# A two-layer recurrent decoder kernel: history rows stacked before they are transposed, unread products of constants on TensorE, and layer norms that scale in one step

## The reference

```
x = layer_norm(ALPHA * x + 0.5 * swiglu(x, ffn1), ln1)
p = x @ w_in
ya, shift, wkv = rwkv7(p[..., :RWKV_COLS], state_shift, state_wkv, ...)
yb, conv, C, n, m = mlstm(p[..., RWKV_COLS:], state_conv, state_C, state_n, state_m, ...)
x = layer_norm(ALPHA * x + concat(ya, yb) @ w_out, ln2)
x = layer_norm(ALPHA * x + 0.5 * swiglu(x, ffn2), ln3)

layer_norm(x, g, b): mu = mean(x); var = mean((x - mu)**2)
                     return (x - mu) * rsqrt(var + LN_EPS) * g + b
```

## Time and profile before

| | |
|---|---|
| runs | 1639.57, 1639.91, 1642.65 us |
| median | 1639.91 us |
| the profiled execution's own time | 1636.58 us |
| its span, first to last instruction | 1634.5 us |
| TensorE busy | 1549.8 us (95%) |
| VectorE, ScalarE, GpSimd busy | 865.3, 665.4, 416.1 us |
| mean granted TensorE clock | 0.965 of 2.4 GHz |

### The profile page before, as it was taken

How to read it: one execution, slowest core, us unless ns; L and a number is a source line. 1 busy time by engine, 2 the same in 40 slices (tenths; PEclk the granted TensorE clock), 3 DMA queues, 4 the chain that set the end, 5 groups by cost and what they waited for, 6 DMA issues and landing times.

```text
span 1634.5 us, 34807 instructions
## 1 busy us (share of the span) xinstructions
PE 1549.8 (95%) x13868; PEld 1486.7 (91%) x13868; DVE 865.3 (53%) x1347; ACT 665.4 (41%) x1071; POOL 416.1 (25%) x427
## 2 busy tenths in 40 slices
PE   7999999999998899999899999999999998999994
PEld 7999998998977799999799999989978787999993
DVE  4444436686356764444464444366944577444334
ACT  4333235656432443333343333357563245333323
POOL 6222552013121432221052221020132324222011
PEclk9999999999997899999999999999999899999997
DMA  7455552442122555544354545434330443544420
GB/s 205 144 151 150 160 152 71 124 112 75 28 62 78 149 147 148 154 143 153 103 147 144 151 143 165 118 96 111 96 76 3 115 119 108 164 143 152 148 97 32
DMA packets 307200, 197.75 MB, mean 121 GB/s; under 512 B 7516, under 2 KB 282320, under 8 KB 307096
## 3 DMA queue, kind: packets, MB, share of 16 engines
q1 hardware_dynamic: 303512, 189.64, 39.9%
q0 software_dynamic: 3584, 6.62, 1.6%
HBM read 187.46 MB, written 8.78 MB: 120 GB/s over the span
## 4 chain that ended last, share of the span: by engine, by line
PE 89%; DVE 5%; ACT 3%; POOL 1%; DVEq 1%; issue 1%; DMA 0%; ACTq 0%; POOLq 0%
PE bank L1905 25%; PE bank L1907 24%; PE bank L1906 24%; PE bank L674 1%; PE bank L690 1%; PE bank L585 1%; PE bank L686 1%; PE bank L561 1%; PE bank L1976 1%; POOL xl L2349 1%; PE bank L423 1%; DVE x L2250 1%; PE bank L1978 1%; PE bank L433 1%; DVE z L2248 1%
## 5 line engine op out<-in xcount | busy, mean ns | idle before, releaser
L1905 PE MATMUL bank<-xh,whi 128*128 128x320 f32 x2016 | 632.8, 314 | 31.6 <-POOL xl L2379 24.7
L2217 DVE TENSOR_TENSOR wlo<-raw,whi 128x1024 fp32r<-128x1024 f32 x340 | 428.2, 1262 | 401.2 <-ACT whi L2101 400.5
L1906 PE MATMUL bank<-xl,whi 128*128 128x320 f32 x2016 | 628.5, 312 | 0.0
L1907 PE MATMUL bank<-xh,wlo 128*128 128x320 f32 x2016 | 628.2, 312 | 0.0
L2101 ACT ACTIVATE whi<-raw 128x1024 fp32r<-128x1024 f32 x340 | 359.2, 1060 | 573.9 <-PE bank L1907 569.4
L1905 PEld LDWEIGHTS bank<-xh,whi 128*128 128x128 f32 x2016 | 383.6, 190 | 38.4 <-issue 32.6
L1906 PEld LDWEIGHTS bank<-xl,whi 128*128 128x128 f32 x2016 | 383.8, 190 | 0.5
L1907 PEld LDWEIGHTS bank<-xh,wlo 128*128 128x128 f32 x2016 | 383.4, 190 | 0.0
L2359 POOL TENSOR_TENSOR hl<-scratch,hh 128x320 f32 x88 | 146.1, 1661 | 435.9 <-DVE scratch L2270 435.9
L1905 PE MATMUL bank<-hh,whi 128*128 (+1 forms) x704 | 218.4, 310 | 0.7 <-ACT vec L2137 0.7
L1907 PE MATMUL bank<-hh,wlo 128*128 (+1 forms) x704 | 217.2, 309 | 0.0
(11 more groups left out here) (363 smaller groups left out, 1568.0 us busy)
## 6 DMA issues: line engine op xcount, KB each, us to landing
raw<-in_ffn_wg SPq DMA_DIRECT2D x88, 512.0 KB, 3.8
raw<-in_ffn_wu SPq DMA_DIRECT2D x88, 512.0 KB, 3.8
raw<-in_ffn_wd SPq DMA_DIRECT2D x88, 512.0 KB, 3.6
raw<-in_w_in SPq DMA_DIRECT2D x60, 512.0 KB, 3.8
raw<-in_w_out SPq DMA_DIRECT2D x16, 512.0 KB, 5.4
raw<-in_state_C SPq DMA_DIRECT2D x8, 512.0 KB, 6.5
out_s_C<-raw SPq DMA_DIRECT2D x8, 512.0 KB, 3.5
ring<-in_state_wkv POOLq DMA_DIRECT2D x2, 1024.0 KB, 8.5
```

The lines of the kernel that those rows point to most:

```text
L1905: pe.matmul(out, w_hi, hi, start=start, stop=False)
L1906: pe.matmul(out, w_hi, lo, start=False, stop=False)
L1907: return pe.matmul(out, w_lo, hi, start=False, stop=stop)
L2217: dve.tensor_tensor(wlo[:, slot, :], raw[:, slot, :], whi[:, slot, :].bitcast(F32), ALU.subtract).then_inc(lo_ready.sem, 1)
```

## The change

Five things change.

1. *Norms.* The matrix of ones in the sums becomes `means`, filled with 1/1024. ACT squares the mean (a new step behind `stats_ready`), DVE makes the variance from it in one operation and floors it in a second. The mean is subtracted from six tiles in three operations of 640 columns. Gain and 1/sqrt are applied in one DVE operation; ACT makes `xh` by adding the bias; DVE, not POOL, makes `xl` in one operation from z, bias and `xh`. x itself is made by ACT, all eight tiles behind the eight of `xh`. For the very last norm no `xh` and `xl` are made.
2. *first_chunks.* PE goes on with six products of a tile as soon as `xh` is there, and makes the three with `xl` one tile later. `gates_product` and `residual` wait for all of x.
3. *Unread products.* `keep_array_busy` makes products of `ident` and `headones` that nobody reads: 18 in each norm but the last of all (4, then 9 behind `var_ready`, then 5 behind `rstd_ready`), and 18 in each layer's recurrence.
4. *History.* It is loaded as 112 and twice 96 rows of 128 and turned by 3 products where 22 stood.
5. *Last rows.* `tails` and `ends` are laid out so that 1 and 2 transposes turn them. The side steps are 24, at growth steps 0 to 5 and 9 to 26, none is left in the recurrence. The stores go out in three conv pieces where two stood.

```diff
+        def keep_array_busy(pe, b, n):
+
+            for _ in range(n):
+                pe.matmul(bank[b][:, 0:P], ident[:, :], headones[:, :], start=True, stop=True)
+
         def gates_product(pe, L):
 
             pe.wait_ge(gatew_in.sem, gatew_in.by(L, 64))
+            pe.wait_ge(xf_ready.sem, xf_ready.by(L, KT))
...
+        SIDE_AT = [*range(KEYS), *range(KEYS + 3, NSIDE + 3)]
...
             if k < VALUES:
-                for i, n in enumerate(range(4 * k, min(4 * k + 4, NRW))):
-                    last = pe.transpose(b[0:SB + 1, i * P:(i + 1) * P], tails[:, n, :], ident[:, :])
+                last = pe.transpose(b[0:(SB + 1) * NRW, 0:P], tails[:, :, :].rearrange("p s n -> p (s n)"), ident[:, :])
...
             elif k < MEMS:
-                for i in range(4):
-                    last = pe.transpose(b[0:LEAD * (SB + 1), i * P:(i + 1) * P],
-                                        ends[:, 4 * (k - ENDS) + i, :, :].rearrange("p s j -> p (s j)"), ident[:, :])
+                for i, (s0_, s1_) in enumerate(END_ROWS):
+                    last = pe.transpose(b[0:(s1_ - s0_) * END_BLOCK, i * P:(i + 1) * P],
+                                        ends[:, s0_:s1_, :, :].rearrange("p s j n -> p (s j n)"), ident[:, :])
...
             for j in range(NJ):
+                keep_array_busy(pe, 7, 2)
                 for b in range(SB):
...
                         samples_u(pe, L)
+                    if c < 3:
+                        keep_array_busy(pe, 7, 2)
...
                 if c == 0:
-                    side(pe, L, NSIDE - 1)
                     left_over(pe, L, NLEFT - 2)
...
                     samples_y(pe, L)
+                if c in (1, 2):
+                    keep_array_busy(pe, 7, 3)
...
-                    for k in range(KT):
-                        pe.wait_ge(x_ready.sem, x_ready.by(L, KT * (which - 1) + k + 1))
-                        for n in range(LOOK):
-                            last = three_passes(pe, outs[n], slot_of(L, base + n), k * P, xh[:, k, :], xl[:, k, :],
-                                                k == 0, k == KT - 1)
-                            if k == KT - 1:
-                                last.then_inc(used.sem, 1)
+                    before = KT * (which - 1)
+                    for k in range(KT + 1):
+                        if k < KT:
+                            pe.wait_ge(xh_ready.sem, xh_ready.by(L, before + k + 1))
+                            for n in range(LOOK):
+                                slot = slot_of(L, base + n)
+                                for w in (whi, wlo):
+                                    pe.matmul(outs[n], w[:, slot, k * P:(k + 1) * P], xh[:, k, :],
+                                              start=(k == 0 and w is whi), stop=False)
+                        if k:
+                            pe.wait_ge(x_ready.sem, x_ready.by(L, before + k))
+                            for n in range(LOOK):
+                                last = pe.matmul(outs[n], whi[:, slot_of(L, base + n), (k - 1) * P:k * P],
+                                                 xl[:, k - 1, :], start=False, stop=(k == KT))
...
+                def through_norm(which):
+
+                    keep_array_busy(pe, 3, 4)
+                    pe.wait_ge(var_ready.sem, var_ready.by(L, which + 1))
+                    keep_array_busy(pe, 3, 9)
+                    pe.wait_ge(rstd_ready.sem, rstd_ready.by(L, which + 1))
+                    keep_array_busy(pe, 3, 5)
...
-                for n in range(NRW):
-                    turn(pe, bank[6][:, n * SB:(n + 1) * SB], hist_shift[:, n * P:(n + 1) * P])
-                for n in range(NQK):
-                    last = turn(pe, bank[7][:, n * 24:(n + 1) * 24], hist_conv[:, n * P:(n + 1) * P])
+                turn(pe, bank[6][:, 0:SB * NRW], hist_shift[:, :])
+                for i in range(2):
+                    last = turn(pe, bank[7][:, i * HALF:(i + 1) * HALF], hist_conv[:, i, :])
...
+                    act.wait_ge(stats_ready.sem, stats_ready.by(L, which + 1))
+                    act.activation(rstd, LN_SUMS[which][0][:, 0:T], ACT.Square).then_inc(msq_ready.sem, 1)
...
-                        g, b = vec[:, g0 + o:g0 + o + 1], vec[:, g0 + KT + o:g0 + KT + o + 1]
-                        act.activation(xh[:, o, :], z[:, o, :], ACT.Identity, scale=g, bias=b).then_inc(
-                            xh_ready.sem, 1)
+                        if not last_norm:
+                            act.activation(xh[:, o, :], z[:, o, :], ACT.Identity,
+                                           bias=vec[:, g0 + KT + o:g0 + KT + o + 1]).then_inc(xh_ready.sem, 1)
+                    for o in range(KT):
+                        act.activation(x[:, o, :], z[:, o, :], ACT.Identity,
+                                       bias=vec[:, g0 + KT + o:g0 + KT + o + 1]).then_inc(xf_ready.sem, 1)
...
+                    dve.wait_ge(msq_ready.sem, msq_ready.by(L, which + 1))
+                    dve.scalar_tensor_tensor(out=var, in0=sums[1], scalar=eps, in1=rstd,
+                                             op0=ALU.add, op1=ALU.subtract)
                     dve.drain()
+                    dve.tensor_scalar(var, var, eps, None, ALU.max).then_inc(var_ready.sem, 1)
+                    dve.tensor_copy(mean, sums[0])
                     dve.drain()
...
+                    for o in range(0, KT - 2, 2):
+                        dve.tensor_tensor(z[:, o:o + 2, :], z[:, o:o + 2, :],
+                                          bcast(mean.rearrange("p (k t) -> p k t", k=1), 1, 2), ALU.subtract)
...
+                        dve.scalar_tensor_tensor(out=z[:, o, :], in0=z[:, o, :], scalar=vec[:, g0 + o:g0 + o + 1],
+                                                 in1=rstd, op0=ALU.mult, op1=ALU.mult).then_inc(norm_ready.sem, 1)
+                        if o + 6 < KT:
+                            dve.tensor_tensor(z[:, o + 6, :], z[:, o + 6, :], mean, ALU.subtract)
                         dve.drain()
-                        dve.tensor_scalar(x[:, o, :], z[:, o, :], g, b, ALU.mult, ALU.add).then_inc(xf_ready.sem, 1)
+                        if o and not last_norm:
+                            low(o - 1)
...
-                        pool.tensor_tensor(xl[:, o, :], x[:, o, :], xh[:, o, :].bitcast(F32), ALU.subtract).then_inc(
-                            x_ready.sem, 1)
```

More of the change, by code:

```diff
@@ L1052, in copy_side @@
             elif k < MEMS:
-                i = k - ENDS
-                last = act.activation(ctail[:, i * 512:(i + 1) * 512], b[0:LEAD * (SB + 1), :], ACT.Copy)
+                for i, (s0_, s1_) in enumerate(END_ROWS):
+                    rows = slice(0, (s1_ - s0_) * END_BLOCK)
+                    last = act.activation(ctail[rows, i, :], b[rows, i * P:(i + 1) * P], ACT.Copy)
             else:
@@ L1968, in ln_sums_of_group @@
                     for out, src in zip(LN_SUMS[which], (zsum, sqsum)):
-                        pe.matmul(out[:, 0:T], ones[:, :], src, start=True, stop=False)
+                        pe.matmul(out[:, 0:T], means[:, :], src, start=True, stop=False)
+                def through_norm(which):
[4 more added lines that the diff above has]
+                    keep_array_busy(pe, 3, 5)
                 def ln_sums(which):
```

130 lines of the change are left out of this document (69 added, 61 removed).

## The result

The changed kernel takes **1630.6 us** (median of 4 runs, 1628.31 to 1635.12), the kernel before in the same session 1639.76 (4 runs). The ratio is 0.9945, with a 95% interval of 0.9924 to 0.9965. It is faster by 9.2 us, where I forecast 1630.3 and a gain of 9.6. The total is right.

What follows compares the result with a forecast made beforehand. TensorE, 89% of the last-ending chain, was taken to bound the kernel through its waits and half clock. 5.8 - 1.4 + 4.2 + 4.0 - 3.0 = 9.6 us off 1639.9 gave 1630.3 us, range 1618 to 1641.

Steps and rivals of the forecast that it cites:

- norm 0 up to the gates, twice: Norm 0, both layers: gates start 17.0 us behind the sums instead of 20.0, gaining 2.9 us each, 5.8 together.
- norms 1 and 2, three stages: Behind norms 1 and 2: 2.0 us gained, 3.4 lost to half clock after the fourth-chunk wait; together a 1.4 us loss.
- last norm: Very last norm: without `xl`, the transposes begin 13.8 us behind the sums instead of 18.1, gaining 4.2 us.
- growth stage, twice (last rows): Growth stage, both layers: fewer last-row transposes and copies gain 2.0 us a layer, 4.0 together.
- recurrence, twice: Recurrence, both layers: the unread products cost more than the better clock returns; 1.5 us lost a layer, 3.0 together.
- third rival: Norms and recurrence: unread products don't hold the clock; gain only 1.5 us, 1638.4 us, no change; chance 0.14.
- The 18 of a norm delay nothing: Each norm's 18 unread products fit into its three waits, delay nothing and hold the clock through the 72 products.
- Eight cost 1.1, bounds 0.5 to 1.7: Recurrence: eight unread products among L730's small products cost 1.1 us a layer, between 0.5 (partly hidden) and 1.7 (full price).
- take half of the gain back: Recurrence: only 2.5 of the 5.0 us a layer from full clock is counted, as the clock may fall again.
- Everything holds: Rival: no clock fall at the fourth chunk, all transposes on the path, recurrence at full clock; gain 21.2, 1618.7 us; chance 0.20.
- The growth stage gives nothing: Rival: ACT's and POOL's steps, not transposes, release the next step there; gain 5.6, 1634.3 us; chance 0.10.
- The slower case: Rival: the recurrence's 18 unread products all run at half clock, 7.7 us a layer; 4.6 slower, 1644.5 us; chance 0.08.

Runs made afterwards that it cites:

- e6: The kernel before with only the stacking of history and last rows; norms, recurrence and unread products as before: 1632.13 us.
- e7: The changed kernel without any unread product, neither in the norms nor in the recurrence: 1621.65 us.
- e1: The changed kernel run again unaltered, for a second profile and the spread: 1630.95 us.
- e5: The changed kernel without the 18 unread products in each norm's wait; those of the recurrence stay: 1628.58 us.
- e12: The changed kernel with the last rows sent out unstacked as before, the history still stacked: 1636.36 us.
- e2: The changed kernel without the 18 unread products of each layer's recurrence; those in the norms stay: 1626.84 us.
- e3: The changed kernel with ScalarE's split of the fourth weight chunk ahead of the eight x writes behind norms 1 and 2: 1627.59 us.
- e8: The changed kernel without the recurrence's unread products and with the fourth chunk's split ahead of the eight x in norms 1 and 2: 1619.10 us.
- e4: The changed kernel with 12 more unread products while TensorE waits for the fourth chunk behind norms 1 and 2: 1630.28 us.
- e10: The kernel of e8 with the eight x of norms 1 and 2 written behind the next stage's first two silu: 1618.97 us.
- e11: The kernel of e8 with the eight unread products of the samples' stage put back in the recurrence: 1622.68 us.

## Why the prediction was right, and where it was not

The sum of 9.6 met 9.2 by luck. The runs take it apart like this: the stacking alone gives 9.2 (e6), the norm edits without unread products 10.5 more (e7), and all unread products together take 10.3 back (e1 against e7). My sum has 4.0, 12.0 (5.8 + 2.0 + 4.2) and a loss of 6.4 (3.4 behind the norms, 3.0 in the recurrence). One gain was too small by 5.2, the other too large by 1.5, and the loss too small by 3.9.

The stages of two profiled executions, gains in us against the kernel before, tell the same by place:

| term | forecast | changed kernel | e1 |
|---|---|---|---|
| norm 0 up to the gates, twice | 5.8 | 5.2 | 5.2 |
| norms 1 and 2, three stages | -1.4 | -4.6 | -3.3 |
| last norm | 4.2 | 4.1 | 4.1 |
| growth stage, twice (last rows) | 4.0 | 2.5 | 5.4 |
| recurrence, twice | -3.0 | -6.1 | -1.0 |
| sum of these | 9.6 | 1.1 | 10.4 |

The spans of these executions gained 1.1 and 12.7 us. Only the norm 0 and last norm terms are the same in both.

Point by point:

- **The norms up to the gates and the last norm: right.** Forecast 2.9 twice and 4.2; the stages show 2.6 twice and 4.1. First product, end of x and the chunk's readiness came within 0.15 us, the wait of 3 us within 0.4. VectorE's subtractions ended 0.45 us behind the exponential (563.42 and 562.97), as forecast.
- **What the norm edits are worth without unread products: the total near, one term not.** e7 and e6 differ by these alone: 10.5 us (19.7 - 9.2). My terms give 3.3 + 2.0 + 4.2 = 9.5 without a held clock (as in the third rival). The stages of the two traces show 3.4, 0.6 and 4.1, so most of the 2.0 for norms 1 and 2 isn't there.
- **"Norms 1 and 2, a loss of 1.4": the direction held, and it is larger.** Where the clock holds behind the wait the three stages take 247.7, 249.0 and 247.7 us, 0.9 less in all than the 745.3 before, for the 2.0 of the sum. Where it falls a stage is 1.4 to 2.8 longer. I had it fall in two of three for 1.7; in the four traces with this wait it fell in 10 of 12.
- **"The 18 of a norm delay nothing": right about delay, wrong about worth.** The first product comes 5.57 us behind the sums with them and 5.56 without (e7). Up to the gates of norm 0 they gain 1.2 us (e5). In norms 1 and 2 they take the half clock out of a place where it cost nothing and put it where it costs. I had written under a rival that the wait for the fourth chunk hides such a loss, and did not ask what that makes of the forecast itself. That all unread products together cost 10.3 us was no case of mine.
- **History and last rows: the size failed.** Forecast 4.0. Measured 9.2 alone (e6) and 5.1 to 5.4 for the last rows taken out of the changed kernel (e12). "The side step moved out of the recurrence: nothing" was wrong: it costs 0.5 to 0.6 us there at an equal clock (e12), and the recurrence became 1.4 and 0.7 shorter in e6. And the growth stage came down by 2.4 and 3.1 us, not 2.0. Part of that is clock (0.96 to 0.98), of which I had no term. "Bounds 0 and 2.9" a layer was too narrow.
- **The recurrence: the size failed.** "Eight cost 1.1, bounds 0.5 to 1.7." The stretch between L800 and L815, with ten unread products in it, took 7.97 us at full clock (485.55 to 493.52); in e7, without them, 4.22, at full clock too (the lines are L799 and L812 there):

```profile
487.35 0.68 PE L799 MATMUL bank<-scratch 64*64 64x64 f32 x16
487.87 3.86 PE L742 MATMUL bank<-scratch 64*64 64x16 f32 x128
491.57 1.04 PE L812 MATMUL bank<-scratch,z 64*64 64x64 f32 x16
...
498.18 0.77 PE L799 MATMUL bank<-scratch 64*64 64x64 f32 x16
```

That is 0.37 us for each, at full clock, above my upper end of 0.215. At the full clock that they bought, L815 to the next L800 took 4.57 us (493.52 to 498.09) for e7's 6.61 at half clock: 2.04 back, with three more unread products in it. Then TensorE waited 2.63 us for VectorE in place of 1.71. Net a loss of 2.5 us up to L761. The clearest pair is e1 and e7:

```profile
480.32:519.04 38.72, 32.33 (x671) 26.08 (x671) 21.71 (x55) 9.96 (x21) 9.54 (x8) 1.00 0.26 70
```

```profile
484.94:521.63 36.69, 31.68 (x634) 26.27 (x635) 21.70 (x55) 9.96 (x21) 9.55 (x8) 0.81 0.27 73
```

With the clock at 1.00 throughout the stage is 2.0 us longer than without unread products at 0.81. In the changed kernel's profiled execution, where it falls to 0.92, it is 4.6 longer. So "take half of the gain back" is refuted: even the whole of it doesn't pay for the products. The clock did rise as forecast (from 0.78 to 0.92 and 1.00). By the medians the whole price of the recurrence's unread products is 4.1 us beside the norms' (e1, e2), 6.9 without the norms' (e5, e7) and 9.4 with the norms' and the split ahead (e3, e8), where I had 3.0. A slip besides: from 110 to 61 ns is 45%, not 43%, 0.2 us a layer.
- **The rule weighed.** The Trainium skill's page TensorE: Matmul & The Clock Gate (section "Wait — 56ns, not 53.3ns?") gives about 62 ns of sequencer time for each matmul when hardware decode is off, a bound where the array's work is shorter. From that I estimated 0.5 us a layer for the eight. A group of sixteen small products with two unread ones ahead takes 1.68 us (486.16 to 487.84), the sixteen alone a quarter of 3.86: the unread ones don't pass beneath the others. That speaks against my use of the page's sentence, not against the sentence.
- **The rivals.** "Everything holds" asked for all clocks held; no execution shows it. "The growth stage gives nothing" is refuted by e6 and e12. "The unread products don't hold the clock" is refuted in the norms (1.00 through the 72 products) and beside the point. The slower case asked for 7.7 us a layer; at most 4.6 was seen.

What stays open: why growth stages of the same code come at 86.7 or near 89.5 us. In the profiled executions, 15 of 24 with stacked rows took at most 87.0 us and the other 9 took 88.3 to 90.7; the four with rows apart took 89.1 to 89.9. The length goes with the granted clock while the number of products stays the same: 86.7 us at 0.98, 88.3 at 0.96, 89.2 to 90.1 at 0.94, 90.7 at 0.92. The longer ones have more stretches of half clock amid dense products. No run here shows what makes the clock fall more often in them, so the missing gain of e4 and e10, most of e11's loss, and the two-way effects in the table stay open.

The version to keep is e8 (or e10, which can't be told from it): 1619.1 us, 22 us faster than before and 12 to 13 faster than the changed kernel.

## What to carry to other kernels

Work that only keeps an engine's clock up must be measured against what the slow clock costs in that place. In this kernel's chain of small products that wait for another engine, full speed shortened TensorE's part and lengthened its next wait (1.71 to 2.63 us), while every added product cost 0.37; and half clock that fell beside a wait that stays was free, so moving it was a loss. Remove the wait first (here by changing the order of two steps on ScalarE), and read gains by stage in several executions, since one profile of this kernel can lie 12 us from the next.

## What the runs showed that I had not expected

- An unread 128x128 float32 product costs 0.26 us back to back in the wait of norm 0 (changed kernel): 36 records, that is 18 products, in 4.68 us:

```profile
257.32 4.68 PE L438 MATMUL bank<-headones,ident 128*128 128x128 f32 x36
```

Between groups of 64x16 products it costs 0.37. Scaling from 320 columns gave 0.215.
- Executions of one kernel on one chip differ by 12 us (1623.5 to 1635.2) with the granted clock between 0.979 and 0.988.
- Stage gains of 4.5 us (e10) can leave the median where it was, and a median can move by 3.6 us (e11) where the stage that was edited moved by 1.1 in both layers together.
